# Cross attention over the memory: a PSUM bank and buffers for each head, both query tiles at once, interleaved with the query and output projections

## The reference, cut to what matters

```python
def memory_cross_attention(h, m, w_q, w_kv, w_o):
    q = einsum('bsd,de->bse', h, w_q).reshape(bsz, seq, 4, 256)
    k, v = split(einsum('bmd,de->bme', m, w_kv), 2, axis=-1)   # each (1, 256, 4, 256)
    s = einsum('bshd,bmhd->bhsm', q, k) * 256 ** -0.5
    p = softmax(s, axis=-1)
    o = einsum('bhsm,bmhd->bshd', p, v).reshape(bsz, seq, 1024)
    return einsum('bsd,de->bse', o, w_o)
```

## Time and profile before

| what | us |
|---|---|
| median of 3 runs | 2060.29 (2059.22 to 2061.13) |
| the profiled execution | 2057.78 |
| its span, first to last instruction | 2056.1 |
| PE busy | 1860.6 (90%) |
| DVE busy | 1338.3 (65%) |
| ACT busy | 907.4 (44%) |
| DMA | 403.93 MB, mean 196 GB/s |
| mean granted TensorE clock | 0.951 |

### The profile page before, as it was taken

The page is one execution under the profiler, slowest core; times in us unless marked ns, Lnnn a source line. Parts: engine busy times, 40 slices in busy tenths (PEclk is TensorE's granted clock), DMA queues, the critical chain, the costliest instruction groups (busy, mean ns, idle before and its releaser), DMA issues.

```text
span 2056.1 us, 25810 instructions
## 1 busy us (share of the span) xinstructions
PE 1860.6 (90%) x10070; PEld 1586.8 (77%) x10070; DVE 1338.3 (65%) x1861; ACT 907.4 (44%) x947; POOL 76.4 (4%) x99
## 2 busy tenths in 40 slices
PE   5999976789799899999999999798967689999997
PEld 2788744678699678999999999697956578878875
DVE  5578675658899465555555555647953478788785
ACT  2543433311233344444444444446533447667664
POOL 0000000000000231111000000000000000000000
PEclk8999998889899999999999999899979889999999
DMA  6555443413345775666555555543334258898892
GB/s 263 224 184 194 144 154 133 164 63 142 113 147 177 237 244 203 211 209 211 187 190 193 184 184 186 197 154 144 123 135 164 92 201 331 327 352 320 317 361 102
DMA packets 60559, 403.93 MB, mean 196 GB/s; under 512 B 7889, under 2 KB 8305, under 8 KB 14017
## 3 DMA queue, kind: packets, MB, share of 16 engines
q1 hardware_dynamic: 51216, 371.22, 48.9%
q0 software_dynamic: 5808, 20.29, 3.4%
q10 hardware_dynamic: 3458, 11.37, 1.7%
HBM read 390.79 MB, written 12.06 MB: 196 GB/s over the span
## 4 chain that ended last, share of the span: by engine, by line
PE 81%; DVE 10%; ACT 4%; issue 3%; DMA 3%; SPq 0%; ACTq 0%; DVEq 0%
PE ps L2054 21%; PE ps L2055 21%; PE ps L2056 21%; PE ps L2132 6%; PE ps L2397 3%; ACT whi L609 2%; DVE wlo L1065 2%; DMA raw<-in_stream_dram 1%; DMA X<-in_x_dram 1%; PE ps L2570 1%; PE ps L2635 1%; PE ps L2456 1%; PE ps L2078 1%; DVE H L1091 1%; PE ps L2271 1%
## 5 line engine op out<-in xcount | busy, mean ns | idle before, releaser
L1065 DVE TENSOR_TENSOR wlo<-raw,whi 128x2048 fp32r<-128x2048 f32 x186 | 426.2, 2292 | 412.5 <-ACT whi L609 412.5
L609 ACT ACTIVATE whi<-raw 128x2048 fp32r<-128x2048 f32 x186 | 356.1, 1915 | 432.7 <-PE ps L2056 407.5
L2054 PE MATMUL ps<-thi,whi 128*128 128x256 f32 x1088 | 311.0, 286 | 5.2 <-DVE tlo L1077 4.2
L2055 PE MATMUL ps<-tlo,whi 128*128 128x256 f32 x1088 | 310.1, 285 | 0.0
L2056 PE MATMUL ps<-thi,wlo 128*128 128x256 f32 x1088 | 309.9, 285 | 0.0
L2054 PE MATMUL ps<-whi,phi 128*128 128x512 f32 x608 | 242.8, 399 | 21.7 <-DVE plo L1617 15.4
L2054 PE MATMUL ps<-whi,thi 128*128 128x512 f32 (+1 forms) x584 | 233.6, 400 | 21.2 <-DVE tlo L1077 15.1
L2055 PE MATMUL ps<-wlo,phi 128*128 128x512 f32 x608 | 240.8, 396 | 0.0
L2056 PE MATMUL ps<-whi,plo 128*128 128x512 f32 x608 | 239.9, 395 | 0.0
L2055 PE MATMUL ps<-wlo,thi 128*128 128x512 f32 (+1 forms) x584 | 229.5, 393 | 0.0
L2056 PE MATMUL ps<-whi,tlo 128*128 128x512 f32 (+1 forms) x584 | 229.4, 393 | 0.0
(11 more groups left out here) (390 smaller groups left out, 2625.6 us busy)
## 6 DMA issues: line engine op xcount, KB each, us to landing
raw<-in_stream_dram SPq DMA_DIRECT2D x264, 1024.0 KB, 4.8
BIG<-in_stream_dram SPq DMA_DIRECT2D x83, 1024.0 KB, 7.2
BIG<-g_spill POOLq DMA_DIRECT2D x64, 128.0 KB, 4.6
BIG<-in_stream_dram SPq DMA_DIRECT2D x2, 2048.0 KB, 15.5
g_spill<-H ACTq DMA_DIRECT2D x4, 1024.0 KB, 4.8
g_spill<-MOD ACTq DMA_DIRECT2D x4, 1024.0 KB, 4.8
MID<-in_gains_dram POOLq DMA_DIRECT2D x7, 512.0 KB, 4.8
s_spill<-MOD ACTq DMA_DIRECT2D x10, 256.0 KB, 4.9
```

Source lines behind the costliest of these rows:

```text
L609: nc.scalar.activation(whi[:, u % 2, :], raw[:, u % 2, :], ACT.Copy).then_inc(unit_hi, 1)
L1065: nc.vector.tensor_tensor(wlo[:, u % 2, :], raw[:, u % 2, :], whi[:, u % 2, :].bitcast(f32), ALU.subtract).then_inc(unit_split, 1)
L2054: nc.tensor.matmul(out, ahi, bhi, start=start, stop=False)
L2055: nc.tensor.matmul(out, ahi, blo, start=False, stop=False)
```

## The change

- Each head `h` has a bank of its own, `ps[:, 4 + h]`, for its scores (both tiles side by side, 512 columns), then its transposes, then its values. `x_p` and `x_pT` have a buffer for each head, and `x_max`, `x_sum`, `x_rec` a column for each head and tile. `pe.wait_ge(x_prob, ...)`, `pe.wait_ge(x_trT, ...)` for shared banks fall away.
- Both tiles go together: one maximum over `128 x 512` for a head instead of two over `128 x 256`, 4 transposes in a row with one copy of 512 columns; `exp` still runs once for each tile, and so does the scaling.
- Scores of head `h` are issued one query group behind their own: group 0, group 1, scores 0, group 2, scores 1, transposes 0, group 3, scores 2, and so on.
- The output projection is taken apart (`rows_part`, one unit for one tile). Its first unit needs the first two heads alone (chunks 0 to 3): tile 0 comes after transposes 2, tile 1 after values 3; the second unit waits for all heads.
- ACT's and DVE's order is written out anew: `hi(U_XO)`, `hi(U_XO + 1)` and their `lo` now stand between the operations of heads.
- `block_rows` is built from `rows_part` and so waits for each tile's bank on its own; it computes what it did. The attention shares semaphores with the differential heads of the first block (`heads_*`), with counts offset by what those add. These renamings are left out below.

```diff
@@ -196,7 +196,7 @@
         lb2, lb, omlb = col(2 * RH), col(RH), col(RH)
 
         warm = col(1)
-        x_max, x_sum, x_rec = col(2), col(2), col(2)
+        x_max, x_sum, x_rec = col(TT * XH), col(TT * XH), col(TT * XH)
         r_stat = col(8 * TT)
 
         big = BIG[:, :]
@@ -311,8 +311,8 @@
         kT = MOD[:, 2048:4096].rearrange("p (b t) -> p b t", b=DC)
         vm = MOD[:, 4096:6144].rearrange("p (t n) -> p t n", t=TT)
         xqT = big[:, 0:2048].rearrange("p (b t) -> p b t", b=DC)
-        x_p = [big[:, 2048 + i * 256:2304 + i * 256] for i in range(2)]
-        x_pT = [big[:, 2560 + i * 512:3072 + i * 512].rearrange("p (k t) -> p k t", k=TT) for i in range(2)]
+        x_p = [big[:, 2048 + h * 512:2560 + h * 512] for h in range(XH)]
+        x_pT = [big[:, 4096 + h * 512:4608 + h * 512].rearrange("p (k t) -> p k t", k=TT) for h in range(XH)]
 
         wr = mid[:, 0:DC * 20].rearrange("p (c n) -> p c n", c=DC)
         r_bias = mid[:, 208:228]
...
@@ -939,31 +938,46 @@
 
             norm(4, X, acc_free, (N_W2 + 3, N_W2 + 4))
             tr_high(T_HX)
-            for u in range(4):
-                hi(U_XQ + u + 2)
-                evac(N_XQ + u, U_XQ + u, xqT[:, 2 * u:2 * u + 2, :].rearrange("p b t -> p (b t)"))
-            def x_exp(i):
-                act.wait_ge(x_bias, i + 1)
-                nc.scalar.activation(x_p[i % 2], ps[:, i % 2, 0:S], ACT.Exp, bias=x_max[:, i % 2:i % 2 + 1],
-                                     scale=XD ** -0.5, accum_out=x_sum[:, i % 2:i % 2 + 1]).then_inc(x_prob, 1)
+            def x_query(h):
+                evac(N_XQ + h, U_XQ + h, xqT[:, 2 * h:2 * h + 2, :].rearrange("p b t -> p (b t)"))
+
+            def x_exp(h):
+                act.wait_ge(x_bias, h + 1)
+                for t in range(TT):
+                    k = TT * h + t
+                    nc.scalar.activation(x_p[h][:, t * S:(t + 1) * S], ps[:, 4 + h, t * S:(t + 1) * S], ACT.Exp,
+                                         bias=x_max[:, k:k + 1], scale=XD ** -0.5, accum_out=x_sum[:, k:k + 1]
+                                         ).then_inc(heads_prob, 1)
+
+            def x_copy(h):
+                act.wait_ge(heads_tr, B_HEADS + h + 1)
+                nc.scalar.activation(x_pT[h].rearrange("p k t -> p (k t)"), ps[:, 4 + h, :], ACT.Copy).then_inc(heads_trT, 1)
 
             def x_out(h):
                 act.wait_ge(xo_full, h + 1)
                 nc.scalar.activation(thi[:, 2 * h:2 * h + 2, :].rearrange("p c t -> p (c t)"),
-                                     ps[:, 6 + h % 2, :], ACT.Copy).then_inc(xo_hi, 1)
-
+                                     ps[:, 4 + h, :], ACT.Copy).then_inc(xo_hi, 1)
+
+            hi(U_XQ + 2)
+            x_query(0)
+            hi(U_XQ + 3)
+            x_query(1)
             x_exp(0)
-            for i in range(XH * TT):
-                h, t = i // TT, i % TT
-                if i + 1 < XH * TT:
-                    x_exp(i + 1)
-                act.wait_ge(x_tr, i + 1)
-                nc.scalar.activation(x_pT[h % 2][:, :, t * P:(t + 1) * P],
-                                     ps[:, 4 + i % 2, 0:S].rearrange("p (k t) -> p k t", k=TT),
-                                     ACT.Copy).then_inc(x_trT, 1)
-                if t == TT - 1 and h:
-                    x_out(h - 1)
-            x_out(XH - 1)
+            hi(U_XO)
+            x_query(2)
+            x_exp(1)
+            x_copy(0)
+            x_query(3)
+            x_copy(1)
+            x_exp(2)
+            x_out(0)
+            x_out(1)
+            hi(U_XO + 1)
+            x_exp(3)
+            x_copy(2)
+            x_copy(3)
+            x_out(2)
+            x_out(3)
             for u in range(U_XO, U_MOE - 2):
                 hi(u + 2)
 
@@ -1830,34 +1844,44 @@
 
             norm(4, X, rows_ready)
             tr_low(T_HX)
-            for u in range(4):
-                lo(U_XQ + u + 2)
-            def x_maxima(i):
-                b = i % 2
-                dve.wait_ge(x_scored, i + 1)
-                mark(nc.vector.tensor_reduce(x_max[:, b:b + 1], ps[:, b, 0:S], axis=AX.X, op=ALU.max))
-                settle()
-                nc.vector.tensor_scalar(x_max[:, b:b + 1], x_max[:, b:b + 1], -(XD ** -0.5), None,
-                                        ALU.mult).then_inc(x_bias, 1)
+            def x_maxima(h):
+                most = x_max[:, TT * h:TT * (h + 1)]
+                dve.wait_ge(heads_scored, B_HEADS + h + 1)
+                mark(nc.vector.tensor_reduce(most, ps[:, 4 + h, :].rearrange("p (t n) -> p t n", t=TT), axis=AX.X, op=ALU.max))
+                settle()
+                nc.vector.tensor_scalar(most, most, -(XD ** -0.5), None, ALU.mult).then_inc(x_bias, 1)
+
+            def x_weights(h):
+                dve.wait_ge(heads_prob, 4 * B_HEADS + TT * (h + 1))
+                mark(nc.vector.reciprocal(x_rec[:, TT * h:TT * (h + 1)], x_sum[:, TT * h:TT * (h + 1)]))
+                settle()
+                for t in range(TT):
+                    last = nc.vector.tensor_scalar(x_p[h][:, t * S:(t + 1) * S], x_p[h][:, t * S:(t + 1) * S],
+                                                   x_rec[:, TT * h + t:TT * h + t + 1], None, ALU.mult)
+                last.then_inc(x_norm, 1)
 
             def x_low(h):
                 dve.wait_ge(xo_hi, h + 1)
                 nc.vector.tensor_tensor(tlo[:, 2 * h:2 * h + 2, :],
-                                        ps[:, 6 + h % 2, :].rearrange("p (c t) -> p c t", c=2),
+                                        ps[:, 4 + h, :].rearrange("p (c t) -> p c t", c=2),
                                         thi[:, 2 * h:2 * h + 2, :].bitcast(f32), ALU.subtract).then_inc(xo_lo, 1)
 
+            lo(U_XQ + 2)
             x_maxima(0)
-            for i in range(XH * TT):
-                b, h, t = i % 2, i // TT, i % TT
-                if i + 1 < XH * TT:
-                    x_maxima(i + 1)
-                dve.wait_ge(x_prob, i + 1)
-                mark(nc.vector.reciprocal(x_rec[:, b:b + 1], x_sum[:, b:b + 1]))
-                settle()
-                nc.vector.tensor_scalar(x_p[b], x_p[b], x_rec[:, b:b + 1], None, ALU.mult).then_inc(x_norm, 1)
-                if t == TT - 1 and h:
-                    x_low(h - 1)
-            x_low(XH - 1)
+            lo(U_XQ + 3)
+            x_weights(0)
+            x_maxima(1)
+            lo(U_XO)
+            x_weights(1)
+            x_maxima(2)
+            x_weights(2)
+            x_low(0)
+            x_low(1)
+            x_maxima(3)
+            x_weights(3)
+            lo(U_XO + 1)
+            x_low(2)
+            x_low(3)
             residual(N_XO, U_XO, 2)
 
 
@@ -2086,22 +2110,27 @@
 
                 return thi[:, c, rows], tlo[:, c, rows]
 
+            def rows_part(n, u, k, t, off=0, uoff=0, at=None, source=rows_of):
+
+                if k == 0:
+                    free_bank(n + t, off)
+                if t == 0:
+                    arrived((u if at is None else at) + k, uoff)
+                s = (u + k) % 2
+                for c in range(4):
+                    rows = slice(t * P, (t + 1) * P)
+                    cols = slice(c * 512, (c + 1) * 512)
+                    ahi, alo = source(4 * k + c, rows)
+                    last = mm3(ps[:, (n + t) % 4, :], ahi, alo, whi[:, s, cols], wlo[:, s, cols],
+                               k == 0 and c == 0, k == 1 and c == 3)
+                if t == TT - 1:
+                    last.then_inc(unit_used, 1)
+
             def block_rows(n, u, off=0, uoff=0, at=None, units=(0, 1), source=rows_of):
 
-                for t in range(TT):
-                    if 0 in units:
-                        free_bank(n + t, off)
                 for k in units:
-                    arrived((u if at is None else at) + k, uoff)
-                    s = (u + k) % 2
                     for t in range(TT):
-                        for c in range(4):
-                            rows = slice(t * P, (t + 1) * P)
-                            cols = slice(c * 512, (c + 1) * 512)
-                            ahi, alo = source(4 * k + c, rows)
-                            last = mm3(ps[:, (n + t) % 4, :], ahi, alo, whi[:, s, cols], wlo[:, s, cols],
-                                       k == 0 and c == 0, k == 1 and c == 3)
-                    last.then_inc(unit_used, 1)
+                        rows_part(n, u, k, t, off, uoff, at, source)
 
             def block_T(out, u, uoff=0):
 
...
@@ -2485,49 +2514,53 @@
 
             transposes(T_HX, H)
             split_rows(T_HX)
-            for u in range(4):
-                group_T(N_XQ + u, U_XQ + u)
-            pe.wait_ge(acc_free, N_XO)
-
-            def x_scores(i):
-                h, t = i // TT, i % TT
-                if i >= 2:
-                    pe.wait_ge(x_prob, i - 1)
-                for c in range(2):
-                    last = nc.tensor.matmul(ps[:, i % 2, 0:S], xqT[:, 2 * h + c, t * P:(t + 1) * P], kT[:, 2 * h + c, :],
```

(60 more changed lines are left out.)

## The result

The changed kernel ran in 2035.22 us (median of 4 runs, 2033.62 to 2040.97) against 2059.76 (4 runs): ratio 0.9887, 95% interval 0.9866 to 0.9908, so 24.5 us less. Timed again in 5 runs, the same kernel took 2038.88 us (2037.83 to 2042.39) against 2058.66 (23 runs, 2052.46 to 2061.56): ratio 0.9910, interval 0.9895 to 0.9924, 19.8 us less. What lies between the two is a large part of what follows.

A forecast was written before the change was run, and what follows sets the result against it. PE was taken as the bound, busy 90% of the span. Removing 21.2 us of waits and half clock, less 0.7 for switching, gave 20.5: 2060.29 - 20.5 = 2039.8 us, range 2036.5 to 2045.5.

The forecast's parts named there:

- The steps of the stage: From query groups to output projection's end, every PE piece finds its operands ready; 21.2 us of waits and slow clock go.
- The thin handovers: In the attention, values 1, projection piece 1, transposes 3, values 3 have 1.0, 0.8, 0.3, 0.9 us of slack.
- The unseen reduction: DVE's maximum over 512 columns, not in the trace, taken as 0.69 us between 0.42 (256) and 1.23 (1024).
- the schedule: Attention's new order laid out piece by piece against old durations at full clock, with PE's end at 1603.8 us.
- the part ahead: Time before the first query matmul: `block_rows` elsewhere put at 0, with at most some tenths of a gain.
- Expert layer shifted as a block by 20.5: Behind the output projection, everything was to start 20.5 us earlier and otherwise stay unchanged.
- the sign of being wrong that the prediction had named: The gap from the output projection's end to the first expert matmul grows.
- The term for switching: PE's changes among some 14 pieces cost 0 to 1.5 us, taken as 0.7 us of loss.
- for what is not seen: Allowance of 2.5 us more gain at the range's lower end, beyond 21.2 us without switching cost.
- No margin failed: First rival, 15%: late ACT or DVE operations make PE wait at thin handovers; typical loss 5 us, 2045.
- no weight was late: Second rival, 4%: expert loads at half rate delay the first expert split; loss 2 to 5 us, 2043.
- The third rival: Clock fails to hold over mixed pieces behind the query groups; 17.6 us slower, 2078; 2%.

The follow-up runs named there:

- the two partial kernels: Changed kernel with the output projection begun only when all four heads are split: 2040.9 us; changed kernel with all query groups before the first scores: 2042.6 us.

## Why the prediction was right and where it was wrong

- **The steps of the stage were right.** No piece of PE came late. The thin handovers kept their slack: transposes 3, projection piece 1, values 1 and values 3 had 0.2, 0.6, 0.9 and 0.9 us against 0.3, 0.8, 1.0 and 0.9 on paper. The unseen reduction was 0.69, and the two partial kernels waited where the schedule said, within 0.2 us.
- **The step that failed: all that lies outside the stage was put at nothing.** The sum took the stage's gain to the end of the kernel as it was. It put the part ahead "at 0, with at most some tenths of a gain", and had the "Expert layer shifted as a block by 20.5". In the first two profiles the parts were 4.7 us less ahead, 21.7 less in the stage and 3.9 more behind, 22.5 in all. The time fell below the range by the part ahead, and that was chance: the same kernel took 1536.5 and 1543.5 us there, with 140.3 and 160.8 us at 1.2 GHz.
- **The part behind is the other half of that step, and it is steady.** It came back to 0.1 us. Of the 3.9 us, 2.0 lie up to the experts' first matmul (31.0 us behind the stage before, 33.1 changed), which is the sign of being wrong that the prediction had named, and 1.9 beyond. In the rest PE had 34.0 us at 1.2 GHz before and 43.5 changed. How fast PE works through the router depends on which of its pieces fall in stretches at 2.4 GHz; ending the stage at another point of that pattern changed it. I had looked at the clock in the stage alone, though the windows behind it could be read as well.
- **The term for switching had the wrong sign.** I excluded a gain from it ("It can't be a gain, since the sum has every piece at its pace") and took 0.7 us of loss. The stage's gain was 21.7, 1.2 more than the 20.5. Eight score records ahead of a query group took 1550.99 - 1549.45 = 1.54 us from start to start, not 8 x 0.215 = 1.72, and four transposes 1559.01 - 1558.66 = 0.35, not 0.56: the next group's first matmul starts in the tail of a piece.
- **The range was too narrow at its lower end.** It allowed 2.5 us "for what is not seen" beyond the stage. The part ahead alone varied from 1536.1 to 1544.5 us over the profiles, and runs of before from 2052.3 to 2067.3; the 95% interval of the first ratio is 4.3 us to either side. The first comparison gave 24.5 us, the second 19.8, where stage and rest give 17.8. The 9 runs of the changed kernel together have the median 2038.8, 1.0 below the forecast of 2039.8; that the forecast's centre fits so well is partly luck, errors of 1.2 and -3.9 us in the sum and the spread of the runs.
- **The rivals.** No margin failed, no weight was late. The third rival had the right mechanism, slow clock behind idle time, in the wrong place and at a tenth of its size: the stage was at 1.00 apart from its first 3 us, the router behind it lost.

## What to carry to other kernels

Where PE waits between small steps of several engines' chains, lay the new order out against old durations piece by piece; here it gave each wait within 0.2 us. Then look at the clock behind the stage that was shortened, not in it alone: a kernel with idle gaps further on can give back several microseconds or get them as a present; here, by the profiles, 0.9 us of useless work took 3.7 us off what followed. Compare the stage's own length in two profiles before believing a difference of medians of four runs.

## What the runs showed of the hardware that was not expected

- The first 400 us, the same work in all kernels, held between 44 and 68 us of clock at 1.2 GHz (51 and 68 in two profiles of one kernel), and the time ahead of the stage went with it by 8 us; from there to the stage the slow time agreed within 3.5 us. Stage and rest of a kernel repeated within 0.1 us although they began at different times of the run.
- The rest took 431.2 to 431.4 us in five kernels whose stages are 63.0 to 83.8 us long, and 433.5 to 435.1 in four others, with the same instructions: a few discrete patterns rather than a spread.
- Matmuls that nothing reads kept the clock up over a wait of 8.0 us, and 32 of them cost nothing on the path; 12 more in a wait of 3.7 us were too many, as the clock had fallen by then. The Trainium skill, "TensorE: Matmul & The Clock Gate", Part 4, has transposes not count as busy PE for the clock. In the stage after, transposes stood in groups of four between matmuls, and the clock there was 1.00; no run here sets transposes apart from the idle time around them, so none shows the rule.
